# Where a convolution's products stand among dense chains, and who makes its taps

## The reference

```python
def conformer_conv(x, w_in, b_in, conv_w, conv_b, ln_g, ln_b, w_out, b_out):
    a, g = jnp.split(x @ w_in + b_in, 2, axis=-1)
    h = a * jax.nn.sigmoid(g)
    h = lax.conv_general_dilated(
        h, conv_w[:, None, :].astype(h.dtype), window_strides=(1,),
        padding=[(CONV_KERNEL - 1, 0)],
        dimension_numbers=("NWC", "WIO", "NWC"),
        feature_group_count=D_MODEL) + conv_b
    h = jax.nn.silu(layer_norm(h, ln_g, ln_b))
    return h @ w_out + b_out
```

## Time and profile before

| | |
|---|---|
| median of 3 runs | 1449.21 us |
| profiled execution, its own time | 1448.2 us |
| its span | 1446.4 us |
| TensorE busy | 1431.5 us, 99% |
| VectorE, ScalarE, GpSimd busy | 916.0, 614.1, 226.5 us |
| convolution stage in the profile | about 911 to 1050 us |

### The profile page before, as it was taken

One profiled execution on the slowest core, in us unless ns is written; L12 is line 12 of the kernel. 1 busy time (PEld: TensorE's weight loads), 2 busy tenths in 40 slices (PEclk: granted clock), 3 DMA queues, 4 the chain that ended last, 5 costly groups with the idle time before them and its releaser, 6 DMA issues. The chain is left out here.

```text
span 1446.4 us, 19981 instructions
## 1 busy us (share of the span) xinstructions
PE 1431.5 (99%) x6878; PEld 1168.8 (81%) x6878; DVE 916.0 (63%) x1324; ACT 614.1 (42%) x914; POOL 226.5 (16%) x172
## 2 busy tenths in 40 slices
PE   8999999999999999999999999899999999999999
PEld 7788888888887898888888888667588888888887
DVE  7877773573655667767754756889888653544532
ACT  5544442342546665444422424667664321222210
POOL 7100000000302231000000003599711000000000
PEclk9999999999999999999999999999999999999999
DMA  5233233233431012332332232249813332332321
GB/s 191 88 102 102 89 101 115 74 101 91 122 102 60 30 60 88 102 102 87 101 117 73 98 101 89 90 111 214 217 45 102 116 102 88 101 102 88 102 95 51
DMA packets 49756, 144.95 MB, mean 100 GB/s; under 512 B 10016, under 2 KB 10784, under 8 KB 49696
## 3 DMA queue, kind: packets, MB, share of 16 engines
q1 hardware_dynamic: 47408, 137.34, 29.7%
q0 software_dynamic: 1440, 5.24, 2.0%
q10 hardware_dynamic: 848, 1.59, 0.3%
HBM read 135.14 MB, written 2.10 MB: 95 GB/s over the span
## 5 line engine op out<-in xcount | busy, mean ns | idle before, releaser
L637 PE MATMUL bank<-xh,whi 128*128 128x512 f32 x1184 | 464.8, 393 | 0.2
L639 PE MATMUL bank<-xh,wlo 128*128 128x512 f32 x1184 | 460.9, 389 | 0.0
L638 PE MATMUL bank<-xl,whi 128*128 128x512 f32 x1184 | 460.8, 389 | 0.0
L1027 ACT ACTIVATE whi<-raw 128x1024 fp32r<-128x1024 f32 x244 | 255.7, 1050 | 245.7 <-PE bank L639 239.0
L1392 DVE TENSOR_TENSOR wlo<-raw,whi 128x1024 fp32r<-128x1024 f32 x230 | 288.7, 1255 | 41.7 <-ACT whi L1027 33.6
L637 PEld LDWEIGHTS bank<-xh,whi 128*128 128x128 f32 x1184 | 222.2, 188 | 54.7 <-issue 6.0
L639 PEld LDWEIGHTS bank<-xh,wlo 128*128 128x128 f32 x1184 | 222.2, 188 | 46.7
L638 PEld LDWEIGHTS bank<-xl,whi 128*128 128x128 f32 x1184 | 222.3, 188 | 46.4 <-issue 1.0
L637 PE MATMUL bank<-ahi,whi 128*128 128x512 f32 x608 | 236.5, 389 | 0.0
L638 PE MATMUL bank<-alo,whi 128*128 128x512 f32 x608 | 236.5, 389 | 0.0
L639 PE MATMUL bank<-ahi,wlo 128*128 128x512 f32 x608 | 236.5, 389 | 0.0
(11 more groups left out here) (196 smaller groups left out, 1313.2 us busy)
## 6 DMA issues: line engine op xcount, KB each, us to landing
raw<-w_ffn_up SPq DMA_DIRECT2D x88, 512.0 KB, 3.3
raw<-w_ffn_down SPq DMA_DIRECT2D x32, 512.0 KB, 3.3
raw<-w_mlp_up SPq DMA_DIRECT2D x32, 512.0 KB, 3.3
raw<-w_mlp_down SPq DMA_DIRECT2D x32, 512.0 KB, 3.3
raw<-w_ain SPq DMA_DIRECT2D x16, 512.0 KB, 3.6
raw<-w_ffn_down SPq DMA_DIRECT2D x16, 384.0 KB, 3.1
raw<-w_qkv SPq DMA_DIRECT2D x12, 512.0 KB, 3.3
raw<-w_wo SPq DMA_DIRECT2D x8, 512.0 KB, 3.4
```

What stands on the lines that cost most here:

```text
L637: nc.tensor.matmul(out_, hi, mh, start=first, stop=False)
L638: nc.tensor.matmul(out_, hi, ml, start=False, stop=False)
L639: return nc.tensor.matmul(out_, lo, mh, start=False, stop=last)
L1027: nc.scalar.activation(whi[:, s, 0:tiles * P], raw[:, s, 0:tiles * P], ACT.Copy)\
```

## The change

**Taps.** TensorE takes 98 of the 248 (86 before), in sets of four shifts for chunks 0 to 6 and of two for chunk 7; the rounds per chunk go from 3, 3, 2, 2, 3, 3, 5, 7 to 3, 2, 2, 3, 3, 3, 5, 7. GpSimd's part falls from 72 to 58. VectorE has 92 (90 before); late taps and the held ones are gone, so that all 92 come ahead of their sets.

**Place.** A set of chunk c stood behind the chains of chunk c+1; now it stands between the two chains of chunk c+2 (behind both for chunks 0 and 5). `OWN_AT_ONCE` says how many of VectorE's taps of a chunk follow its own gating; the others follow the gating of the next chunk.

**Low parts.** GpSimd computes those of units 6 and 7 only; those of 8 and 9 are made by adding transfers as well, and the places at which GpSimd issues them are new.

```diff
-PE_TAPS = (6, 6, 8, 8, 12, 12, 20, 14)
-SHIFTS = (2, 2, 4, 4, 4, 4, 4, 2)
+PE_TAPS = (12, 8, 8, 12, 12, 12, 20, 14)
+SHIFTS = (4, 4, 4, 4, 4, 4, 4, 2)
...
-STATS_AFTER = 2
-COLLECT_AT = 3
+STATS_AFTER = 3
+COLLECT_AT = 8
+BETWEEN = range(3, C - 1)
...
-POOL_TAPS = (11, 10, 10, 9, 9, 9, 8, 6)
-LATE_TAPS = (2, 8, 10, 12, 9, 0, 0, 0)
...
+POOL_TAPS = (10, 9, 8, 8, 7, 7, 5, 4)
+OWN_AT_ONCE = (3, 4, 4, 2, 5, 7, 6)
+EVICT_AT = (3, 0, 0, 0, 0, 2, 1)
...
-POOL_LOW = (6, 7, 8, 9)
+POOL_LOW = (6, 7)
...
-                for k in (2 * (c % 2), 2 * (c % 2) + 1) if c else ():
-                    chain(p, c // 2, k, xh, xl)
-                if 1 <= c <= HELD:
-                    convolve(c - 1)
-                if c == C - 1:
-                    convolve(HELD)
+                if c:
+                    chain(p, c // 2, 2 * (c % 2), xh, xl)
+                if c in BETWEEN:
+                    convolve(c - 2)
+                if c:
+                    chain(p, c // 2, 2 * (c % 2) + 1, xh, xl)
+                if c >= 2 and c not in BETWEEN:
+                    convolve(c - 2)
                 if c >= 3:
                     statistics(c - 3)
...
             for c in range(C):
+                if c >= 3:
+                    square(c - 3)
                 act.wait_ge(hc_ready, c + 2)
...
+                products(c, range(2 if c == 0 else 0, min(GATE_PRODUCTS, POOL_TAPS[c])))
+                if c < C - 1:
                     sigmoid(c + 1)
...
+                if 1 <= c < C - 2:
+                    split_hi(p.unit, 0, 2 * (c + AHEAD))
+                    if 2 * (c + AHEAD) in ADDED:
+                        negate_high(2 * (c + AHEAD))
+                products(c, range(GATE_PRODUCTS, POOL_TAPS[c]))
...
+                if c < C - 3:
+                    split_hi(p.unit, 0, 2 * (c + AHEAD) + 1)
+                    if 2 * (c + AHEAD) + 1 in ADDED:
+                        negate_high(2 * (c + AHEAD) + 1)
...
+                gated(c)
...
+                    last = own_taps(c - 1)
+                    for n in range(OWN_AT_ONCE[c - 1], len(last)):
+                        own_tap(c - 1, n, last[n])
...
+                    if EVICT_AT[c] == 0:
+                        evict(c + 1, 0)
+                    if c >= 2:
+                        collect(c - 2)
                     diagonals(c)
```

More of the change, by code:

```diff
@@ L50 @@
 QUADRANT = P // 4
-GATE_AT = 8
-STATS_AFTER = 2
-COLLECT_AT = 3
+STATS_AFTER = 3
+COLLECT_AT = 8
+BETWEEN = range(3, C - 1)
 R1_CHUNKS = (3, 4, 5, 6)
-R1_AT = 3
 DIAGS = 2
-POOL_TAPS = (11, 10, 10, 9, 9, 9, 8, 6)
-LATE_TAPS = (2, 8, 10, 12, 9, 0, 0, 0)
-HELD = C - 3
-HELD_TAPS = 7
-LATE_START = (2, 2, 2, 0, 0, 0, 0, 0)
+POOL_TAPS = (10, 9, 8, 8, 7, 7, 5, 4)
+OWN_AT_ONCE = (3, 4, 4, 2, 5, 7, 6)
+EVICT_AT = (3, 0, 0, 0, 0, 2, 1)
 PARTS = 9
-GATE_PRODUCTS = 6
+GATE_PRODUCTS = 5
 HC = 3
-LOW_AT = {6: (0, 7), 7: (0, 9), 8: (1, 5), 9: (1, 7), 10: (2, 5), 11: (2, 7), 12: (3, 5), 13: (3, 7), 14: (4, 5), 15: (4, 7), 16: (5, 6), 17: (7, 1), 18: (7, 3),
-          19: (7, 5)}
+LOW_AT = {6: (0, 6), 7: (0, 9), 8: (1, 1), 9: (1, 3), 10: (1, 6), 11: (2, 1), 12: (2, 5), 13: (3, 1), 14: (3, 5), 15: (4, 1),
+          16: (5, 3), 17: (6, 3), 18: (7, 3), 19: (7, 3)}
 OTHER_LOW = tuple(LOW_AT)
-POOL_LOW = (6, 7, 8, 9)
+POOL_LOW = (6, 7)
 ADDED = tuple(e for e in LOW_AT if e not in POOL_LOW)
@@ L320, in build @@
         tap_steps = sem("tap_steps")
-        late_steps = sem("late_steps")
         own_added = sem("own_added")
@@ L349, in own_taps @@
         def own_taps(c):
-            return range(PE_TAPS[c] + POOL_TAPS[c], TAPS - LATE_TAPS[c])
+            return range(PE_TAPS[c] + POOL_TAPS[c], TAPS)
         def o_at(t, s):
@@ L1333, in _ @@
             for c in range(C):
+                if c >= 3:
+                    square(c - 3)
                 act.wait_ge(hc_ready, c + 2)
[L1335 to L1341, removed]
-                    sigmoid(c + 1)
[L1343 to L1355, removed]
+                if c == 0:
+                    products(c, range(2))
+                    split_hi(p.unit, 0, AHEAD + 2)
+                products(c, range(2 if c == 0 else 0, min(GATE_PRODUCTS, POOL_TAPS[c])))
+                if c < C - 1:
+                    sigmoid(c + 1)
+                if 1 <= c < C - 2:
[3 more added lines that the diff above has]
+                products(c, range(GATE_PRODUCTS, POOL_TAPS[c]))
+                if c == 0:
+                    split_hi(p.unit, 0, 2 * AHEAD)
+                if c < C - 3:
+                    split_hi(p.unit, 0, 2 * (c + AHEAD) + 1)
+                    if 2 * (c + AHEAD) + 1 in ADDED:
+                        negate_high(2 * (c + AHEAD) + 1)
                 if c == C - 2:
@@ L1358, in _ @@
                     negate_high(17)
-            square(C - 2)
+            square(C - 3)
             split_hi(p.unit, 0, 18)
             negate_high(18)
+            square(C - 2)
             nc.scalar.activation(eps[:, 4:5], eps[:, 0:1], ACT.Sqrt)
@@ L1751, in own_tap @@
                                        op0=ALU.mult, op1=ALU.add).then_inc(tap_steps, 1)
[L1753 to L1760, removed]
             def diagonals(c):
@@ L1790, in collect @@
                     dve.wait_ge(own_added, 1)
-                dve.wait_ge(late_steps, sum(LATE_TAPS[:c + 1]))
                 dve.wait_ge(conv_done, c + 1)
@@ L1827, in _ @@
                     evict(0, 0)
-                if c < C - 1:
-                    gated(c)
-                if c < C - 1:
-                    diagonals(c)
[L1833 to L1849, removed]
-                        evict(c + 1, 0)
[L1851 to L1858, removed]
+                own = own_taps(c)
@@ new lines, in _ @@
+                if c == C - 1:
+                    collect(C - 3)
+                    for n, k in enumerate(own):
+                        if n == COLLECT_AT:
+                            collect(C - 2)
+                        own_tap(c, n, k)
+                    continue
+                gated(c)
+                if c == 0:
+                    split_lo(p.unit, 0, AHEAD + 1)
+                else:
+                    last = own_taps(c - 1)
+                    for n in range(OWN_AT_ONCE[c - 1], len(last)):
+                        own_tap(c - 1, n, last[n])
+                    if c == 1:
+                        diagonals(0)
+                    if EVICT_AT[c] == 0:
+                        evict(c + 1, 0)
+                    if c >= 2:
+                        collect(c - 2)
+                    diagonals(c)
@@ L1859, in _ @@
+                for n in range(OWN_AT_ONCE[c]):
+                    if n and n == EVICT_AT[c]:
+                        evict(c + 1, 0)
+                    if c == 0 and n == 2:
+                        split_lo(p.unit, 0, AHEAD + 2)
+                        evict(1, 0)
+                    own_tap(c, n, own[n])
+                if c in R1_CHUNKS:
+                    invert_residual(R1_CHUNKS.index(c))
                 if c == C - 2:
```

4 lines of the change are left out of this document (removed).

## The result

The changed kernel takes 1458.45 us (median of five executions, 1456.19 to 1459.56) where the kernel before took 1447.33 beside it (1446.86 to 1451.06): a ratio of 1.0067, 95% interval 1.0056 to 1.0079 (the ratio weighs all executions; that of the two medians is 1.0077). It is slower, by 8 to 11 us; the forecast was 4.8 us slower. The profiled execution of it took 1457.04, its span is 1455.3 us, 8.9 over the span before.

The account below looks back on a forecast made before the run. TensorE, busy in 99% of the run, was taken as the bound, its gaps in the convolution stage worth 9.1 us. 14.0 us added less 9.1 gave 4.9, said as 4.8 slower: median 1454.0 us, range 1446.5 to 1459.5.

Parts of the forecast that it names:

- What the change takes away: TensorE, chunk 0's set and chunk 3's copy: wait 5.94, slow clock 2.59 and copy wait 0.52 go, 9.1 us.
- GpSimd's 24 us less buy no time by themselves: GpSimd loses 14 additions and two splits, 24 us, but only has to be in time for VectorE's gathering.
- the bound read from TensorE's gaps alone: TensorE's gaps between 911 and 1050 us: it can win back 9.1 us and not more, 0.6%.
- Part 1, the squares: Statistics of chunks 0 to 2 wait for ScalarE's high part, negation and square: 2.93 us three times, 8.8 us added.
- Part 2, the taps: Sets wait for VectorE's taps behind the next chunk's gating: chunk 1 1.3, chunk 2 1.2, sum 2.5 us added.
- The clock: TensorE's clock behind three new 2.9 us waits: one fall in three taken, 0.8 us added, bounds 0 to 7.8.
- Rival (a): TensorE's clock falls at every new wait: +11.9 us, 1461; chance 0.12.
- Part 3 and the end: More changes between large and small matmuls, 0.8 us; TensorE's wait for the last statistics, 1.1 us; both added.
- DMA, zero: More shifted copies and adding transfers, put where the DMA share was 0.42: zero, up to 3 us if late.
- rival (b): DMA becomes the bound once two adding transfers per chunk run: 3 us for unit 8 or 9, 1457; chance 0.10.
- Rival (c): ScalarE's wait is hidden, VectorE's waits of 9.1 us come in its place: +1.9, 1451.1; chance 0.10.
- Rival (d): GpSimd paced the stage, so its relief lets ScalarE and VectorE run ahead: faster, 1442; chance 0.08.

Follow-up runs that it names:

- e6: The kernel before with fourteen of GpSimd's taps, and their fourteen products on ScalarE, left out of the computation: 1451.12 us, ratio 1.0018.
- e4: The kernel before with eight of VectorE's twelve taps of chunk 0 left out of the computation: 1449.29 us, ratio 1.0008.
- e7: The kernel before with both GpSimd's fourteen taps and eight of VectorE's taps of chunk 0 left out: 1444.17 us, ratio 0.9976 to the kernel before.
- e8: The changed kernel with squares and VectorE's taps early, and TensorE taking twelve taps of chunk 1 instead of eight: 1444.98 us, ratio 0.9982 to the kernel before.
- e5: The changed kernel with twelve more unread matmuls in each of TensorE's four long waits: 1453.36 us, ratio 1.0034 to the kernel before.
- e2: The changed kernel with ten more of VectorE's taps of chunks 2 to 4 right behind their own gating: 1459.77 us, ratio 1.0078 to the kernel before.
- e9: e8 with ScalarE's squares of chunks 0 to 2 one more place ahead, before the rest of the products: 1442.44 us, ratio 0.9963 to the kernel before.
- e11: The changed kernel with the sets of chunks 1 to 4 behind both chains instead of between them: 1453.22 us, ratio 1.0044 to the kernel before.
- e12: e11 with VectorE's taps early as in e2 and the squares at the place of e9: 1442.18 us, ratio 0.9965 to the kernel before.
- e1: The changed kernel with ScalarE's squares of chunks 0 to 2 moved ahead of the high part they stood behind: 1455.97 us, ratio 1.0051 to the kernel before.
- the two edits: ScalarE's squares earlier (e1) and VectorE's taps earlier (e2), each alone on the changed kernel: 1455.97 and 1459.77 us.
- e3: The changed kernel with both edits, ScalarE's squares and VectorE's taps earlier: 1444.97 us, ratio 0.9982 to the kernel before.

## Why the prediction was right, and where its sizes were off

The direction and the mechanism held: slower, inside the range of 1446.5 to 1459.5, by the waits that it named. Its size did not: the median is 4.4 us over the forecast of 1454.0 and 1 us inside the end of the range, and the highest execution, 1459.56, is past it. Step by step:

- *What the change takes away, 9.1 us:* right in the trace after. A wait of 0.43 us for copies at chunk 7's set went too, and was not in the sum. But that GpSimd's 24 us less buy no time by themselves was half the truth. They buy none (e6), yet in the kernel before, the removal of VectorE's wait bought none without them either (e4), and both together 3.9 us (e7). So the bound read from TensorE's gaps alone was no bound for one engine's relief; GpSimd's 94.39 of 100 us were the sign. That the changed kernel, with its other order, needed GpSimd's relief too is argued from these runs and not shown.
- *Part 1, the squares:* 2.93 us three times forecast, 2.91 three times measured. The order of the instructions and three durations were enough for it.
- *Part 2, the taps:* chunk 2's 1.2 was 1.22. **Chunk 1's 1.3 was 2.86, the first term mis-sized.** The 2.02 us between the last matmul of the chain and the first tap came from a place where VectorE was free; here it was still at the first taps of the same chunk, and the eviction began at 947.44, 2.04 behind 945.40, so that the ten taps began 3.62 behind it: 1.6 more, which is the difference. The taps stood 0.79 apart again ((7.88 - 0.75) / 9), so the row was the right guide. The sentence of the Trainium skill (VectorE: DVE Perf Modes, "The DRAIN you can't avoid") that a semaphore costs nothing extra rests on copies, with a semaphore after each or only after the last. The prediction stretched it: the taps 0.66 and those 0.79 apart all signal a semaphore, and only those 0.79 apart also wait for the tap just before, so the rows put the 0.13 us on that and don't contradict the sentence. e8 shows that this wait goes with four taps fewer.
- *The clock:* **0.8 us was the second mis-sized term, and the larger.** It was 3.2 in the profiled execution and up to 5.1 by the medians of e5 and the changed kernel. I had reckoned with one fall in three waits, and had left VectorE's waits out; two of four long waits were followed by one. Rival (a), a fall at every new wait, didn't happen either.
- *Part 3 and the end:* 0.8 and 1.1 forecast, 1.3 and 0.69 measured; the former is only what the account leaves over.
- *DMA, zero:* no set or chain of the changed kernel waits for a transfer, so rival (b) didn't happen. The transfers were close behind: in e2, e5, e8, e9, e11 and e12 ScalarE waits 1.06 to 3.56 us for the raw weights of unit 11, as soon as TensorE comes to that place 1 to 3 us earlier.
- *Rival (c)* is what e1 made: without the squares' waits VectorE's take their place, at the sizes given. *Rival (d)* is refuted by the changed kernel itself, in which the waits of parts 1 and 2 stand with GpSimd relieved, and by e6, which is no faster.

The two terms, 1.6 and 2.4, are 4.0 of the 4.0 us by which the profiled span (8.9) went past the sum (4.9). The rest of the medians' difference may be the clock too: the highest execution has the lowest mean clock (1459.56 at 0.993), but 1459.12 and 1456.19 both have 0.995, so it isn't shown.

## What to carry to other kernels

A wait behind another engine's late step hides that of the next: ask of each wait taken away who is second in line and at what size, and expect little from relieving one engine alone where a second is nearly as late (2.5 us and none for the two edits by themselves, 13.5 for both). An instruction that others wait for must not stand behind one that waits for the consumer itself: here a square of 0.6 us, placed behind a high part whose slot the running chain was reading, cost 2.9 us three times. A gap of 3 us on TensorE has to be priced with what the clock may take behind it, by the executions and not by a single profile.

## What the runs showed of the hardware that was not expected

The same wait of 2.86 or 2.87 us, at the same place, was followed by different clocks: the set behind it, 1.93 us at full clock, took 3.20, 2.76, 1.93 and 3.43 us in the profiled executions of the changed kernel, e1, e2 and e3. With matmuls whose results nobody reads in the same four gaps the clock was at 1.00 throughout (e5), even over the 2.55 us that stayed idle there. A kernel with the longer order of work can therefore be the faster one: e5 does 48 matmuls more than the changed kernel and is 5.1 us faster by the medians.
